# Input projection by token groups, with the gates and the sixteen mixer chunks between its slabs

## What is computed

```python
proj = x @ w_in                      # 1024 -> 22 tiles of 128 columns, and 8 gate columns
i_pre = softcap(mi + b_ig); f_pre = softcap(mf + b_fg)         # gates, per token and head
# group A: mLSTM, 4 heads of 128, a state (C, n, m) carried from chunk to chunk
qk  = (q k^T) * exp(logD - m_row)
num = sc * (q C) + qk v;  den = sc * (q n) + sum(qk)
h   = num / max(|den|, exp(-m_row));  C_new = a * C + kw^T v
h_ml = h * rsqrt(mean(h*h) + eps) * ml_g * sigmoid(mo)
# group B: attention over a window of 128, 8 query heads, 2 kv heads, sinks, relative bias
s = q k^T / 8 + bias;  p = exp(s - mx) / (sum + exp(sink - mx));  o = p v
x = LayerNorm(alpha * x + concat(h_ml, o) @ w_out)
x = LayerNorm(alpha * x + SwiGLU(x))                            # 1024 -> 2 x 2816 -> 1024
```

## Time and profile before

| | us |
|---|---|
| median of 3 runs | 2705.39 |
| profiled execution, first to last instruction | 2705.0 |
| start, until the first product | 12.4 |
| projection | 522.7 |
| gates, loads of chunks 0 and 1 | 34.6 |
| chunk 0, to its store | 32.6 |
| chunks 1 to 15, to the last store | 247.8 |
| sample stage and layer | 1854.9 |

### The profile page before, as it was taken

One profiled execution on the slowest core, in us unless ns is written; L12 is line 12 of the kernel. 1 busy time (PEld: TensorE's weight loads), 2 busy tenths in 40 slices (PEclk: granted clock), 3 DMA queues, 4 the chain that ended last, 5 costly groups with the idle time before them and its releaser, 6 DMA issues.

```text
span 2705.0 us, 39819 instructions
## 1 busy us (share of the span) xinstructions
PE 2549.0 (94%) x14173; PEld 2466.6 (91%) x14173; DVE 1062.1 (39%) x1723; ACT 798.0 (30%) x1270; POOL 1082.2 (40%) x462
## 2 busy tenths in 40 slices
PE   8999999958888779999999999999999999999996
PEld 8999999847776779999999999999999999999996
DVE  4111111147776243333553325644157341563403
ACT  2000000047885124422332223322224222242221
POOL 1111111012223335555455554555545555455553
PEclk9999999979998779999999999999999999999998
DMA  4212111176675314433344332443324433343332
GB/s 160 96 63 76 65 72 69 48 174 151 151 151 147 113 58 141 139 115 115 108 153 142 114 124 95 148 149 120 119 96 134 167 118 116 102 127 116 119 118 68
DMA packets 164636, 314.91 MB, mean 116 GB/s; under 512 B 16124, under 2 KB 111060, under 8 KB 161092
## 3 DMA queue, kind: packets, MB, share of 16 engines
q1 hardware_dynamic: 162224, 305.34, 36.3%
q10 hardware_dynamic: 2340, 8.52, 1.1%
HBM read 270.80 MB, written 44.17 MB: 116 GB/s over the span
## 4 chain that ended last, share of the span: by engine, by line
issue 39%; POOL 14%; PE 11%; DVE 1%; POOLq 1%; DMA 0%; ACT 0%; DVEq 0%
POOL l_wlo L1390 14%; PE l_acc L1512 4%; PE l_acc L1514 4%; PE l_acc L1513 4%; POOLq L1387 1%; DVE nrm L1641 0%; DVE stats L1632 0%; DMA out_y<-nrm 0%; POOLq L1389 0%; PE turned L1532 0%; DVE nrm L1739 0%; DVE nxt L1654 0%; DVE nxt L1650 0%; POOL al L1397 0%; DVE mv L1635 0%
## 5 line engine op out<-in xcount | busy, mean ns | idle before, releaser
L1390 POOL TENSOR_TENSOR l_wlo<-l_raw,l_whi 128x1024 fp32r<-128x1024 f32 (+1 forms) x338 | 906.4, 2682 | 848.9 <-ACT l_whi L1419 848.9
L1512 PE MATMUL l_acc<-ah,l_whi 128*128 128x416 f32 x2080 | 733.3, 353 | 23.6 <-DVEq L1613 9.9
L1514 PE MATMUL l_acc<-ah,l_wlo 128*128 128x416 f32 x2080 | 735.6, 354 | 0.0
L1513 PE MATMUL l_acc<-al,l_whi 128*128 128x416 f32 x2080 | 728.4, 350 | 0.0
L1419 ACT ACTIVATE l_whi<-l_raw 128x1024 fp32r<-128x1024 f32 (+1 forms) x338 | 384.9, 1139 | 1134.0 <-PE l_acc L1514 1100.8
L1512 PEld LDWEIGHTS l_acc<-ah,l_whi 128*128 128x128 f32 x2080 | 392.0, 188 | 29.0 <-POOL l_wlo L1390 10.3
L1513 PEld LDWEIGHTS l_acc<-al,l_whi 128*128 128x128 f32 x2080 | 392.4, 189 | 6.3
L1514 PEld LDWEIGHTS l_acc<-ah,l_wlo 128*128 128x128 f32 x2080 | 391.6, 188 | 2.7
L1512 PE MATMUL l_acc<-hh,l_whi 128*128 128x416 f32 x880 | 311.4, 354 | 7.5 <-POOL l_wlo L1390 2.9
L1514 PE MATMUL l_acc<-hh,l_wlo 128*128 128x416 f32 x880 | 309.9, 352 | 0.0
L267 PE MATMUL acc<-xh,whi 128*128 128x416 f32 x880 | 309.3, 351 | 0.0
(11 more groups left out here) (295 smaller groups left out, 2413.0 us busy)
## 6 DMA issues: line engine op xcount, KB each, us to landing
l_raw<-in_wB SPq DMA_DIRECT2D x260, 512.0 KB, 3.4
l_raw<-in_w SPq DMA_DIRECT2D x80, 704.0 KB, 4.1
projT<-out SPq DMA_DIRECT2D x22, 1040.0 KB, 4.0
inp<-projT SPq DMA_DIRECT2D x16, 1280.0 KB, 6.7
raw<-in_wA SPq DMA_DIRECT2D x22, 512.0 KB, 5.4
xraw<-in_xT SPq DMA_DIRECT2D x10, 832.0 KB, 4.6
mixr<-mixT SPq DMA_DIRECT2D x5, 1664.0 KB, 8.9
nxt<-in_xT SPq DMA_DIRECT2D x5, 1664.0 KB, 7.8
```

Source lines behind the costliest of these rows:

```text
L1390: nc.gpsimd.tensor_tensor(wlo[:, s, 0:k], raw[:, s, 0:k], whi[:, s, 0:k].bitcast(F32), ALU.subtract).then_inc(S["lo_done"], 1)
L1512: pe.matmul(acc[:, bank, 0:TG], whi[:, s, c], hx[:, a], start=(a == 0), stop=False)
L1513: pe.matmul(acc[:, bank, 0:TG], whi[:, s, c], lx[:, a], start=False, stop=False)
L1514: last = pe.matmul(acc[:, bank, 0:TG], wlo[:, s, c], hx[:, a], start=False, stop=(a == total - 1))
```

## The change

`project`, `gates` and `prompt` become one block, `mixers`, unrolled, with one numbered step for each of 126 values of n. `sample` and `layer` follow as before.

- **Projection.** It goes over the token groups instead of the weights: 110 slabs of one group each (n = 0 to 109), slab n being tile n mod 22 of group n div 22. Only two groups' x is held (`xh0`, `xl0`, `xh1`, `xl1`); the weights are read from DRAM again for each group, x is read in 8 visits instead of 5: one visit for each of the five gate products, which stand ahead of slabs 0, 3, 6, 9 and 12, and three more for groups 2 to 4. `whi` and `wlo` have three buffers, `raw` two, `out` three of one group each; two PSUM banks are used for the products. Each slab and group has its own store to `projT`.
- **Gates.** Their steps stand behind slabs 5 and 13 to 21, one link of the chain to a slab.
- **Chunks.** A chunk is cut in six pieces that stand behind six slabs in a row: TURN (first window scores, turns of keys and values, scores), MIX (turned window 0 and 1, heads, state update), WIN (window scores 2 and 3, values 0 and 1), TURN2, VALUES, OUT. The chunks begin at n = 24, 29, 34, 46, 51, 56, 68, 73, 78, 90, 95, 100, 105, 110, 115, 120: chunk c+1's TURN stands with chunk c's OUT, and nothing else of two chunks overlaps. From n = 110 on there is no slab between the pieces. Loads of the chunks stand at the n of `LOADS_AT`; where a chunk is the first that needs a new group, its load waits until that group's last stores have landed.
- Buffers are placed by hand (`Store` with an offset); the gates' buffers and the chunks' share one place.

The core of the diff (functions as they are in the new kernel; what is cut is the same as in the old one or of the same pattern):

```diff
+NSLAB = NG * NPROJ
+GATES = 5
+GATE_EVERY = 3
+VISITS = ((0, 0), (4, 1), (3, 1), (2, 1), (1, 1), (2, 0), (3, 1), (4, 0))
+SPLIT_AT = (None, (0, 1), (3, 4), (6, 7), (9, 10), (25, 28), (47, 50), (69, 72))
+LOAD_X_AT = (None, None, (1, 2), (4, 5), (7, 8), (14, 15), (32, 33), (54, 55))
+BASES = (24, 29, 34, 46, 51, 56, 68, 73, 78, 90, 95, 100, 105, 110, 115, 120)
+PIECES = tuple(tuple(range(b, b + 6)) for b in BASES)
+TURN, MIX, WIN, TURN2, VALUES, OUT = range(6)
+LOADS_AT = (21, 22, 28, 43, 44, 50, 65, 66, 72, 87, 88, 93, 98, 109, 110, 113)
...
+        @block.sync
...
+            for n in range(END):
+                if n < NSLAB:
+                    if n % GATE_EVERY == 0 and n // GATE_EVERY < GATES:
+                        store_gates(n // GATE_EVERY)
+                    if n + 4 < NSLAB:
+                        sp.wait_ge(lo_done, n + 3)
+                        load(n + 4)
+                    store(n)
...
+                for c in range(NC):
+                    if LOADS_AT[c] == n:
+                        load_chunk(c)
+                for c in at_piece(n, OUT):
+                    store_chunk(c)
...
+        @block.tensor
...
+            def turn(c):
+                s = c % 2
+                pe.wait_ge(loaded[s], c // 2 * 64 + 64)
+                wait(pe, "sq_ready", c)
+                if c:
+                    wait(pe, "pt_copied", c - 1, 4)
+                window_scores(c, 0)
+                wait(pe, "ml_mixed", c - 1)
...
+            def mixed(c):
+                turn_window(c, 0)
+                turn_window(c, 1)
+                wait(pe, "v_copied", c)
+                wait(pe, "p_ready", c)
+                wait(pe, "qs_ready", c)
+                wait(pe, "st_ready", c - 1)
...
+            for n in range(END):
+                if n < NSLAB:
+                    if n % GATE_EVERY == 0 and n // GATE_EVERY < GATES:
+                        i = n // GATE_EVERY
+                        product(gate_tile(i), ghi, glo, i, True)
+                    slab(n)
...
+                for c in at_piece(n, OUT):
+                    turn_out(c)
+                for c in at_piece(n, TURN):
+                    turn(c)
+                for c in at_piece(n, MIX):
+                    mixed(c)
+                for c in at_piece(n, WIN):
+                    window(c)
+                for c in at_piece(n, TURN2):
+                    turn_window(c, 2)
+                    turn_window(c, 3)
+                for c in at_piece(n, VALUES):
+                    values(c)
...
+        @block.scalar
...
+            def round_slab(n):
+                act.wait_ge(raw_in[n % 2], n // 2 * 16 + 16)
+                if n >= 3:
+                    act.wait_ge(acc_full, slab_tile(n - 3) + 1)
+                nc.scalar.activation(whi[:, n % 3], raw[:, n % 2], ACT.Copy).then_inc(hi_done, 1)
...
+            def turned(c):
+                s = c % 2
+                wait(act, "v_turned", c)
+                wait(act, "state_up", c - 1)
+                nc.scalar.activation(vaug[:, :, 0:P], ce[:, 0].rearrange("p (h e) -> p h e", e=P), ACT.Copy).then_inc(S["v_copied"], 1)
+                window_exp(c, 0)
+                wait(act, "e_ready", c)
+                wait(act, "u_ready", c)
+                wait(act, "kw_ready", c - 1)
+                for h in range(H):
+                    last = nc.scalar.activation(decay[:, h], expo[:, h], ACT.Exp, bias=ucol[:, s, h:h + 1])
+                last.then_inc(S["d_exp"], 1)
+                window_exp(c, 1)
+                wait(act, "ml_mixed", c - 1)
+                nc.scalar.activation(gate[:], inp[:, s, MO:MO + 4], ACT.Tanh, scale=0.5).then_inc(S["tanh_ready"], 1)
...
+            for n in range(END):
+                if n + 3 < NSLAB:
+                    round_slab(n + 3)
```

More of the change, by code:

```diff
@@ L370, in gates, with slab_tile, gate_tile, mixers @@
+END = PIECES[-1][OUT] + 1
+def slab_tile(n):
+    return n + 1 + min(n // GATE_EVERY, GATES - 1)
+def gate_tile(i):
+    return (GATE_EVERY + 1) * i
+def mixers(nc, io, keep, outs, taken, at):
+    cols, sbias, ident = keep["cols"], keep["sbias"], keep["ident"]
     R = H * NC
     with ExitStack() as ctx:
-        m = Store(nc, ctx)
-        tile = lambda n: (m.sb(n, [R, C]), m.sb(n + "_s", [H, NS]))
-        gi, gf, gis, gfs, small, small_s, m0, loaded = (
-            gate_in[n] for n in ("gi", "gf", "gi_s", "gf_s", "small", "small_s", "m0_sb", "loaded"))
+        m = Store(nc, ctx, at)
+        xh, xl = [], []
+        for b in range(2):
+            if b:
+                second = Store(nc, ctx, keep["second_at"])
+            s = second if b else m
+            xh.append(s.sb(f"xh{b}", [P, KD, TG], F32R))
+            xl.append(s.sb(f"xl{b}", [P, KD, TG], F32R))
+        xraw = m.sb("xraw", [P, 2, XK, TG])
+        raw = m.sb("raw", [P, 2, KD, P])
+        whi = m.sb("whi", [P, 3, KD, P], F32R)
+        wlo = m.sb("wlo", [P, 3, KD, P], F32R)
+        out = m.sb("out", [P, 3, TG])
+        inp = m.sb("inp", [P, 2, 20, C])
+        kwin = m.sb("kwin", [P, 2, 2 * W])
+        svT = m.sb("svT", [P, 2, W])
+        xs = m.sb("xs_b", [P, 2, H, 2, C])
+        bias = m.sb("bias", [P, 8, 2 * W])
+        bias_prev = m.sb("bias_prev", [P, 8, W])
+        state, nlast, mix, mix_out, kv_out, st_out = (outs[n] for n in ("state", "nlast", "mix", "mix_out", "kv_out", "st_out"))
+        causal = m.sb("causal", [P, C])
+        ones = m.sb("ones", [P, 1])
+        sinks = m.sb("sinks", [P, 8])
+        gml = m.sb("gml", [P, H])
+        zeros = m.at
+        t = Store(nc, ctx, zeros)
+        g = {n: t.sb(n, s) for n, s in (
+            ("gi", [R, C]), ("gf", [R, C]), ("gi_s", [H, NS]), ("gf_s", [H, NS]),
+            ("small", [R, 4]), ("small_s", [H, 4]), ("m0_sb", [H, DB]))}
+        g["loaded"] = t.sem("g_loaded")
+        gi, gf, gis, gfs, small, small_s, m0, g_loaded = (
+            g[n] for n in ("gi", "gf", "gi_s", "gf_s", "small", "small_s", "m0_sb", "loaded"))
+        tile = lambda n: (t.sb(n, [R, C]), t.sb(n + "_s", [H, NS]))
@@ new lines, in mixers @@
+        own = t.sb("own", [R, C])
+        gx, gxs = t.sb("xs", [R, 2, C]), t.sb("xss", [H, 2, NS])
+        ones_r = t.sb("ones_r", [R, C])
+        m_last = t.sb("m_last", [H, DB])
+        m_end = t.sb("m_end", [1, H])
+        ends = t.sb("ends", [1, 2, H, NC])
+        after = t.sb("after", [1, H, NC])
+        before = t.sb("before", [1, H, NC])
+        inherited = t.sb("inherited", [R, 1])
+        anti = t.sb("anti", [P, P])
+        hank = t.sb("hank", [P, 8, 2 * W])
+        srow = t.sb("srow", [32, 132])
@@ new lines, in load_chunk @@
+            def load_chunk(c):
+                s, tok = c % 2, slice(c * C, c * C + C)
+                if c >= 2:
+                    for n in ("win", "qs_ready", "tanh_ready", "st_ready"):
+                        wait(sp, n, c - 2, each[n])
+                if c in (0, 3, 6, 9, 13):
+                    last = slab_tile((0, 3, 6, 9, 13).index(c) * NPROJ + NPROJ - 1)
+                    for k in range(last - 2, last + 1):
+                        landed(k)
+                sp.dma_start(inp[:, s], io["projT"][0:20, :, tok].rearrange("t p n -> p t n")).then_inc(loaded[s], 16)
+                if c:
+                    sp.dma_start(kwin[:, s], io["projT"][SK, :, c * C - W:c * C + C]).then_inc(loaded[s], 16)
+                else:
+                    sp.dma_start(kwin[:, s].rearrange("p (a k) -> p a k", a=2),
+                                 bass.AP(tensor=io["projT"].tensor, offset=SK * P * NT, ap=[[NT, P], [0, 2], [1, W]])).then_inc(loaded[s], 16)
+                sp.dma_start(svT[:, s], io["projT"][SV, :, tok]).then_inc(loaded[s], 16)
+                sp.dma_start(xs[:, s].rearrange("p h w n -> p (h w) n"),
+                             bass.AP(tensor=io["xsT"].tensor, offset=c * C, ap=[[0, P], [NT, 2 * H], [1, C]])).then_inc(loaded[s], 16)
@@ new lines, in _ @@
+            nc.gpsimd.memset(glo[:].bitcast(F32), 0.0).then_inc(g_zero, 1)
+            pool.wait_ge(g_hi, 1)
+            pool.wait_ge(g_zero, 2)
+            nc.gpsimd.tensor_tensor(glo[:, :, 0:8], graw[:], ghi[:, :, 0:8].bitcast(F32), ALU.subtract).then_inc(g_split, 1)
+            for n in range(3):
+                rest(n)
+            nc.gpsimd.memset(ones_r[:], 1.0).then_inc(gq, 1)
+            nc.gpsimd.memset(before[:], 0.0).then_inc(gq, 1)
+            nc.gpsimd.memset(bias[:, :, 0:W], NEG).then_inc(gq, 1)
@@ L722, in window_scores, with slab @@
+            def slab(n):
+                gr = n // NPROJ
+                pe.wait_ge(lo_done, n + 1)
+                product(slab_tile(n), whi[:, n % 3], wlo[:, n % 3], (0, 4, 5, 6, 7)[gr], n % NPROJ == 0)
+            def window_scores(c, r):
+                s = c % 2
+                for gr in range(2):
+                    gp = slice(64 * gr, 64 * gr + 64)
                     for a in range(2):
-                        last = pe.matmul(w01[:, g, a * 256:a * 256 + 256], sq8[gp, r + a], kwin[gp, s],
```

(17 more changed lines are left out.)

1158 lines of the change are left out of this document (514 added, 644 removed).

## The result

The changed kernel takes 2776.24 us (median of 4 runs) against 2706.18 us of the kernel before beside it: ratio 1.0259, 95% interval 1.0245 to 1.0274. It is slower; 2671 us was predicted.

What follows compares the result with a forecast made beforehand. TensorE was taken as the bound, busy 2549.0 of 2705.0 us. Terms reached 729.8 us at slab 109's end and 816.0 after the tail; with 1854.9 unchanged, 2671 us was forecast (2650 to 2692, chance 0.60).

Steps and rivals of the forecast that it cites:

- Start, products, gates: Projection and gates: first product at 10.2 us, 1.8 lost at low clock, 115 products 521.0, gates adding 3 and 1.
- Chunks behind slabs: Pieces between slabs: 13.2 us of TensorE slots a chunk plus 0.3, 168.7 us for thirteen, and 4 for small waits.
- The timing of MIX behind TURN: Tightest place in a chunk behind slabs: ScalarE done at 7.9 us, TensorE arriving at 8.2 + 0.5, under 1 us to spare.
- Rival 3: Pieces don't fit: three of each chunk wait 1 us for ScalarE or VectorE, 39 us, 2710 us; chance 0.06.
- Weights: "I take nothing": Weight slabs read five times: a raw buffer's round just fits in 9.06 us, three whi in reserve, so no loss added.
- the weights queued behind both come about 3 us before they are needed: Weight tiles in the queue behind two chunks' loads were claimed to arrive in time, about 3 us early.
- Loads of chunks: TURN's waits for chunk data: 6.7 us at chunk 0, 2.8 each (8.4) at chunks 3, 6 and 9.
- Rival 2: Weights come too late in the 42 bare slabs: 90 us less 20 of swallowed load stalls, 2741 us; chance 0.11.
- The tail: After slab 109: 16.6 us until chunk 13's TURN, 3 for low clock, three bare chunks of 21.7, ending at 816.0.
- rival 1: Tail stays at the low clock: matmuls of the three bare chunks double, 25 us more, 2696 us; chance 0.13.
- The ring rule: Chunk loads on SP's queue: descriptors consumed in ring order, so a weight tile behind a chunk's load waits for all of it.
- The sentence that closes the sum: Whole mixers block: of 34.6 + 16 us around the gates and 3.3 x 13 of hidden waits, about 30 are given back.

Runs made afterwards that it cites:

- the order's run: Changed kernel with ScalarE rounding a slab after the step's chunk pieces and GpSimd preparing a chunk before subtracting, DMAs unmoved: 2718.51 us, ratio 1.0046 to before.
- the queue's run: Changed kernel with weight tiles from slab 4 on loaded by DMAs that ScalarE issues on its own queue, ahead of its rounding: 2707.95 us, ratio 1.0003 to before.

## Why the prediction was wrong, step by step

- *Start, products, gates.* Near. The first product starts at 10.53 (10.2 predicted), bare slabs are 4.53 apart, and slab 24's copy comes at 160.9, 4 us behind the 156.9 that follows from the sum (10.2 + 1.8 + 30 products + 9).
- *Chunks behind slabs.* The slots of 13.2 us came out (35.9 us for five slabs and a chunk), but with some luck: the terms listed for a slot add up to 14.0, not 13.2, and with 14.0 the sum would have been 10 us longer. Away from the ten intervals next to nothing waits in the pieces: TensorE is busy for all 35.90 us from 245.77 to 281.67. The timing of MIX behind TURN, with its small margin, held. Rival 3 didn't happen.
- *Weights: "I take nothing".* This step failed. I asked when TensorE needs a tile and found three slabs of reserve. I didn't ask who stands behind the rounding on ScalarE. In the new order that is the chunk's own work, so the reserve was not there for the chunk: a tile is needed at the rounding, three slabs before its product. In the kernel before, the roundings of the projection had no chunk's work behind them. The sentence "the weights queued behind both come about 3 us before they are needed" was good enough for TensorE (in the order's run no product waits for a tile) and useless for ScalarE. Of the 84 us that the sum lacked, 7.5 are the chunks' own loads (next item) and about 77 stand here, with what the low clock after the waits adds to them; the queue's run, where tiles no longer stand behind SP, is 69 us shorter at these intervals.
- *Loads of chunks.* The 6.7 us for chunk 0 were near, the 2.8 us each for chunks 3, 6 and 9 too small. In the changed kernel the chunks' rows land 7.1, 3.5, 3.6 and 6.0 us after the copy of the slab ahead of TURN; with 0.6 for the query scaling the four waits make 22.6 us where 15.1 were in the sum. With the weights on a queue of their own the intervals are still 14.3, 15.6, 14.9 and 17.2, that is 6.2, 7.5, 6.8 and 9.1 us over 8.1. Of the 99 us that the ten intervals are too long, the order alone takes away 52 and the queue alone 69; two slabs more of cover bring another 20 us of the kernel's time.
- *Rival 2* had the sign and the size of the result (2741 us), but not the place: it priced bare slabs late for TensorE. These ran at 4.5 us, as the layer had said. I gave the right transfer the wrong waiter, and that its 2741 us lie nearest the measured time is luck.
- *The tail.* The wait for chunk 13's load was near (18.8 for 16.6). The bare chunks were rival 1: I gave 0.13 to a low clock, and it was there. The granted clock is 0.68 in these 84.6 us, and the 16 us that warm matmuls bring stand beside the 25 priced. My ground against it was that chunks at 16.52 us held the clock at 1.00; those overlapped, these have more gaps, none longer than 2.3 us. In chunk 13 of the changed kernel, on TensorE:

```profile
843.68 0.63 PE L492 MATMUL w<-ident,pw 128*128 128x128 f32 x4 [1.76 <-ACT pw L640]
845.83 1.09 PE L492 MATMUL w<-ident,pw 128*128 128x128 f32 x4 [1.52 <-ACT pw L640]
...
859.09 3.68 PE L501 MATMUL fb<-vs,ptw 128*128 128x64 f32 x16 [1.38 <-ACT ptw L650]
```

  Four matmuls take 0.63 us where the granted clock is 1.00, 2.4 GHz (842 to 844 us), and 1.09 where it is 0.50, 1.2 GHz (845 to 847), two us apart. The Trainium skill (TensorE: Matmul & The Clock Gate, HAM oscillation) says that idle gaps between bursts bring the clock down again and again; the trace agrees in the result, though its gaps here are short.
- *The ring rule*, that descriptors are consumed in ring order (the Trainium skill, DMA: Bandwidth & Descriptors, Queues, rings and completion order), agrees with one queue here: slab 27's tile, issued 0.5 us after the rows of chunk 1, landed about 1 us after them (185.4 and 184.2). But a second queue did not bring tiles in quickly (worst landing 12.5 us for 13.9). The same section says that the rings of both queues lie on the same 16 DMA engines; the trace agrees, with these engines busy all the time from 162 to 170 us of that run (DMA share 1.11 and 1.03). The queue freed the issue from SP's own waits.
- The sentence that closes the sum, that about 30 us are given back, doesn't fit its own items: 16.6, 16 and the stalls of 28 make some 60, and it is the gain of 34 that is left. The total is not touched by it.

## What to carry to other kernels

When work of two kinds is interleaved by hand, go through each engine's stream and ask of every waiting instruction what stands behind it, not only when its result is needed. Put prefetch work (a rounding three slabs ahead) behind the work that is due now, or issue its transfer from a queue that isn't held up by large loads. And give a stretch that falls out of the interleaving its own check of the clock; matmuls without a reader brought back 14 us here, while 72 of them ahead of one piece held it up by as much once its data came earlier.

## What the runs showed of the hardware

- SP's issue of a DMA of 128 KB (`kwin`) takes 2.5 to 3.4 us behind one chunk's `inp` in most places. Where a second chunk's load follows right behind the first it takes 5.7 to 9.5 us in the changed kernel, 9.95 in the kernel before. The next issue of SP comes only after that (in the lines above the tile at 171.54).
- GpSimd's subtraction on 128x64 takes 1.88 us beside VectorE's split of x, and the 16 times larger one alone 2.40: 

```profile
8.60 1.88 POOL L420 TENSOR_TENSOR glo<-graw,ghi 128x64 fp32r<-128x64 f32 x1 [6.01 <-ACT ghi L700]
```

  It ends at 10.48, 0.2 us behind the split (8.40 + 1.89 = 10.29), and the first product waits for it. So the small `glo` brought the start forward only about to the point that x allowed anyway.
- Three bare chunks whose gaps on TensorE are all under 2.3 us have a mean granted clock of 0.68 and take 84.6 us; with fillers in some of the gaps they have 0.95 and take 68.2.
